# First layer's dilated q and k accumulated in one place, causal q with its cross terms apart: a change to a two-layer hybrid decoder kernel

## The reference, cut to what matters

```
h = rms_norm(x, attn_norm)
proj = h @ w_in
qa, ka, va, qd, kd, vd = jnp.split(proj, [...], axis=-1)
qa = apply_rope(split_heads(qa, N_HEADS_MOBA), cos, sin)
qd = apply_rope(split_heads(qd, N_HEADS_DIL), cos, sin)
x = x + jnp.concatenate([out_a, out_d], axis=-1) @ w_out
x = x + jnp.square(jax.nn.relu(h @ w_up)) @ w_down
```

## Time and profile before

| | us |
|---|---|
| median of three runs | 595.81 |
| profiled execution | 595.47 |
| its span in the trace | 593.7 |
| PE busy in the span | 583.4 (98%) |
| DVE busy | 403.0 (68%) |
| ACT busy | 314.1 (53%) |
| layer 0, step 8 starts | 20.12 |
| layer 0, quad of heads 4 to 7 starts | 57.94 |
| layer 1, the same quad starts | 346.66 |

### The profile page before, as it was taken

How to read it: one execution, slowest core, us unless ns; L and a number is a source line. 1 busy time by engine, 2 the same in 40 slices (tenths; PEclk the granted TensorE clock), 3 DMA queues, 4 the chain that set the end, 5 groups by cost and what they waited for, 6 DMA issues and landing times.

```text
span 593.7 us, 9303 instructions
## 1 busy us (share of the span) xinstructions
PE 583.4 (98%) x3350; PEld 491.6 (83%) x3350; DVE 403.0 (68%) x650; ACT 314.1 (53%) x532; POOL 61.8 (10%) x67
## 2 busy tenths in 40 slices
PE   8989999999999999999999999999999999999995
PEld 6869977788888888888888888778888888888884
DVE  5795987688755755755388968768775755656634
ACT  5746767475535435435185646774645435435322
POOL 0060240210000000000004214102000000000001
PEclk9999999999999999999999999999999999999999
DMA  8946352448665465564255625441876465564301
GB/s 305 368 145 212 106 177 76 139 142 275 221 217 206 148 220 198 154 249 163 71 174 181 213 98 187 143 142 44 270 243 223 151 229 185 158 235 172 107 0 71
DMA packets 58844, 104.20 MB, mean 176 GB/s; under 512 B 1808, under 2 KB 35136, under 8 KB 58816
## 3 DMA queue, kind: packets, MB, share of 16 engines
q1 hardware_dynamic: 58320, 103.03, 51.6%
q10 hardware_dynamic: 496, 0.81, 0.5%
HBM read 102.79 MB, written 1.05 MB: 175 GB/s over the span
## 4 chain that ended last, share of the span: by engine, by line
PE 92%; DMA 3%; DVE 3%; issue 1%; ACT 0%; POOLq 0%; ACTq 0%; POOL 0%; DVEq 0%; SPq 0%
PE psum L1172 20%; PE psum L955 16%; PE psum L957 16%; PE psum L956 16%; PE psum L1175 10%; PE psum L976 5%; DMA raw<-in_w_in 3%; PE psum L981 3%; PE psum L1107 2%; PE psum L1127 2%; PE psum L1145 1%; PE psum L962 1%; DVE w_lo L670 1%; PE psum L1148 1%; DVE rope_b L736 0%
## 5 line engine op out<-in xcount | busy, mean ns | idle before, releaser
L670 DVE TENSOR_TENSOR w_lo<-raw,w_hi 128x1024 fp32r<-128x1024 f32 x188 | 227.2, 1242 | 51.3 <-ACT w_hi L498 51.3
L498 ACT CAST w_hi<-raw 128x1024 fp32r<-128x1024 f32 x188 | 186.7, 1048 | 1.7 <-DMA raw<-in_w_in 1.2
L1172 PE MATMUL psum<-xt,w_hi 128*128 128x512 f32 x512 | 160.7, 395 | 0.0
L955 PE MATMUL psum<-w_hi,ot_hi 128*128 128x512 f32 x320 | 127.0, 397 | 0.0
L956 PE MATMUL psum<-w_lo,ot_hi 128*128 128x512 f32 x320 | 124.8, 390 | 0.0
L957 PE MATMUL psum<-w_hi,ot_lo 128*128 128x512 f32 x320 | 124.8, 390 | 0.0
L1175 PEld LDWEIGHTS psum<-xt,w_lo 128*128 128x128 f32 x512 | 96.2, 188 | 22.4
L1175 PE MATMUL psum<-xt,w_lo 128*128 128x256 f32 x512 | 100.6, 278 | 0.0
L1172 PEld LDWEIGHTS psum<-xt,w_hi 128*128 128x128 f32 x512 | 80.2, 189 | 2.4
L614 ACT COPY up_cross<-psum 128x512 f32<-128x512 f32 x32 | 18.8, 587 | 118.8 <-PE psum L1175 118.8
L846 DVE TENSOR_TENSOR up_cross<-psum,up_cross 128x512 f32<-128x512 f32 x32 | 22.1, 691 | 74.1 <-ACT up_cross L614 74.1
(11 more groups left out here) (98 smaller groups left out, 609.3 us busy)
## 6 DMA issues: line engine op xcount, KB each, us to landing
raw<-in_w_up SPq DMA_DIRECT2D x32, 1024.0 KB, 5.5
raw<-in_w_down SPq DMA_DIRECT2D x32, 1024.0 KB, 6.8
raw<-in_w_in SPq DMA_DIRECT2D x21, 1024.0 KB, 5.2
raw<-in_w_out SPq DMA_DIRECT2D x8, 1024.0 KB, 4.9
raw<-in_w_in SPq DMA_DIRECT2D x3, 512.0 KB, 7.9
raw<-in_w_in SPq DMA_DIRECT2D x4, 256.0 KB, 4.7
out<-x SPq DMA_DIRECT2D x3, 256.0 KB, 2.4
x<-in_x SPq DMA_DIRECT2D x2, 256.0 KB, 4.4
```

The source lines that it names most:

```text
L498: act.copy(dst, src).then_inc(hi_done, 1)
L670: dve.tensor_tensor(lo_t, src, hi_t, ALU.subtract).then_inc(split_done, 1)
L955: pe.matmul(out, s_hi, m_hi, start=first, stop=False)
L1172: pe.matmul(up_banks[b][:, f, :], w_hi[:, slot, cols[f]], xt[:, k, :, :].rearrange("p a b -> p (a b)"), start=k == 0, stop=False)
```

## The change

Layer 0's groups 0 and 1 (dilated q and k) are accumulated in one place: three matmuls of 256 columns a tile and k (`together`), no copies of cross terms, no `add_cross`, rope products straight from PSUM. Layer 1's groups 0 and 1 stay as they were. Group 3 (causal q) has its cross terms apart in both layers: 512 and 256 columns into banks 0 and 1 for half 0, 2 and 3 for half 1, with a copy by ACT and an `add_cross` by DVE at steps 28 and 32.

What moves with it: the row of 1/rms is turned at step 9 into bank 7 instead of at step 11 into bank 0; rope products of dilated q go to steps 10 and 12, of causal q from 28 and 32 to 29 and 33; head 5 is masked at step 30 instead of 31, and so turned at 33 instead of 34; heads 4 and 5 are scored in banks 0 and 1 instead of 1 and 2; two `hi` of ACT come earlier (31 to 29, 32 to 30). PE's waits change with the banks.

```diff
-QK_STEPS = [19, 21, 23, 25, 29, 31, 33, 35, 43, 44, 45, 46, 48, 49, 50, 51]
+QK_STEPS = [19, 21, 23, 25, 29, 30, 33, 35, 43, 44, 45, 46, 48, 49, 50, 51]
...
-CROSS_AT = {8: ((0, 0), (0, 1)), 12: ((1, 0),), 16: ((1, 1),), 36: ((4, 0),), 40: ((4, 1),)}
-SUM_AT = {8: (0, 0), 9: (0, 1), 14: (1, 0), 16: (1, 1), 36: (4, 0), 40: (4, 1)}
-ROPE_ROW = 11
-ROPE_AT = {12: (0, 0), 13: (0, 1), 14: (1, 0), 17: (1, 1), 28: (3, 0), 32: (3, 1), 37: (4, 0), 41: (4, 1)}
+LATER_CROSS = {28: ((3, 0),), 32: ((3, 1),), 36: ((4, 0),), 40: ((4, 1),)}
+CROSS_AT = [LATER_CROSS, {8: ((0, 0), (0, 1)), 13: ((1, 0),), 16: ((1, 1),)} | LATER_CROSS]
+LATER_SUMS = {28: (3, 0), 32: (3, 1), 36: (4, 0), 40: (4, 1)}
+SUM_AT = [LATER_SUMS, {8: (0, 0), 9: (0, 1), 14: (1, 0), 16: (1, 1)} | LATER_SUMS]
+ROPE_ROW = 9
+ROPE_AT = {10: (0, 0), 12: (0, 1), 14: (1, 0), 18: (1, 1), 29: (3, 0), 33: (3, 1), 37: (4, 0), 41: (4, 1)}
...
-HI_LATE = {28: 3, 30: 2}
-HI_AT = {s + HI_LATE.get(s, int(s % 8 in (0, 4))): s // 2 + HI_AHEAD for s in range(0, 2 * ATT_UNITS, 2)}
+HI_AT = {s + int(s % 8 in (0, 4)): s // 2 + HI_AHEAD for s in range(0, 2 * ATT_UNITS, 2)}
...
-            return banks[(1, 2, 4, 5)[h % 4]]
+            return banks[(1, 2, 4, 5)[h % 4] - int(h in (4, 5))]
...
-            warm_up(4)
-            for n in range(4):
-                pe.matmul(banks[n][:, :], squares[:, 0, BANK:BANK + P], squares[:, 1, 0:BANK], start=True, stop=False)
+            warm_up(8)
...
-            def half_in_one_bank(hg, i, k, slot):
-
-                out = group_bank(3, hg)[:, i * SEQ:(i + 1) * SEQ]
-                return three(out, feature_tile(w_hi, k, slot, hg, i), feature_tile(w_lo, k, slot, hg, i),
-                             xt[:, k, 0, :], xt[:, k, 1, :], k == 0, k == KT - 1)
+            def together(g, k, slot, hg, i):
+
+                return three(qk_banks(g, hg)[:, i, 0:SEQ], feature_tile(w_hi, k, slot, hg, i),
+                             feature_tile(w_lo, k, slot, hg, i), xt[:, k, 0, :], xt[:, k, 1, :], k == 0, k == KT - 1)
...
-                    if g == 2 and half == 0:
+                    if g == 1 and half == 1:
                         pe.wait_ge(rope_scaled, l + 1)
+                    elif g == 2:
+                        pe.wait_ge(rope_terms, qk_half(l, 0, half) + 1)
                     elif g == 3:
                         pe.wait_ge(v_done, l * 4 + half + 1)
+                        pe.wait_ge(masked, l * N_HEADS + half + 1)
+                    elif g == 4 and half == 0:
+                        pe.wait_ge(masked, l * N_HEADS + 6)
                     elif g == 4:
-                        pe.wait_ge(rope_terms, qk_half(l, 3, half) + 1)
-                        pe.wait_ge(masked, l * N_HEADS + 4 + half + 1)
+                        pe.wait_ge(acc_summed, APART[l, 3, 1] + 1)
                     elif g == 5:
-                        pe.wait_ge(acc_summed, l * len(SUMMED) + SUMMED[4, half] + 1)
+                        pe.wait_ge(acc_summed, APART[l, 4, half] + 1)
...
+                    elif (l, g, half) in APART:
+                        last = both_tiles(g, k, slot, half)
                     else:
-                        last = both_tiles(g, k, slot, half)
+                        for i in range(2):
+                            last = together(g, k, slot, half, i)
...
+                if h == 4:
+                    pe.wait_ge(acc_summed, APART[l, 3, 0] + 1)
...
             def attention(l, s):
                 if s == ROPE_ROW:
                     pe.wait_ge(rstd_done, l * STATS + ST_X + 1)
-                    pe.wait_ge(acc_summed, l * len(SUMMED) + 1)
```

More of the change, by code:

```diff
@@ L567, in _ @@
                                        scale=rstd[:, ST_X, t:t + 1]).then_inc(v_done, 1)
-                    for g, hg in CROSS_AT.get(s, ()):
+                    for g, hg in CROSS_AT[l].get(s, ()):
                         if g > 0 and hg == 0:
@@ L802, in _ @@
                         norm(l, NORM_AT[s])
-                    if s in SUM_AT:
-                        add_cross(l, *SUM_AT[s])
+                    if s == ROPE_ROW:
+                        scale_rope(l)
+                    if s in SUM_AT[l]:
+                        add_cross(l, *SUM_AT[l][s])
                     if s in ROPE_AT:
-                        if s == min(ROPE_AT):
-                            scale_rope(l)
                         rope_products(l, *ROPE_AT[s])
@@ L938, in _ @@
             pe.sem_inc(pv_done, 4)
-            pe.wait_ge(ones_set, 2)
+            pe.wait_ge(ones_set, 1)
             def warm_up(n):
@@ L1005, in first_project_in @@
                     pe.matmul(qk_banks(0, hg)[:, i, 0:SEQ], feature_tile(w_hi, k, slot, hg, i), xt[:, k, 0, :],
-                              start=False, stop=False)
+                              start=k == 0, stop=False)
                 if k % 2 == 0:
@@ L1011, in first_project_in @@
                 for hg, i in tiles:
-                    with_lo(0, k, slot, hg, i)
+                    pe.matmul(qk_banks(0, hg)[:, i, 0:SEQ], feature_tile(w_lo, k, slot, hg, i), xt[:, k, 0, :],
+                              start=False, stop=False)
                 pe.wait_ge(turned_lo, k + 1)
                 for hg, i in tiles:
-                    last = pe.matmul(qk_banks(0, hg)[:, i, SEQ:2 * SEQ], feature_tile(w_hi, k, slot, hg, i),
+                    last = pe.matmul(qk_banks(0, hg)[:, i, 0:SEQ], feature_tile(w_hi, k, slot, hg, i),
                                      xt[:, k, 1, :], start=False, stop=False)
@@ L1025, in project_in @@
                 half, j = s % 8 // 4, s % 4
-                if half == 0 and g == 3 and j < 2:
-                    unit_ready(l, 2 * g + j, 1)
-                elif half == 0 and g != 3:
+                if half == 0:
                     unit_ready(l, 2 * g + j // 2, j % 2)
                 if j == 0:
-                    if g == 2 and half == 0:
+                    if g == 1 and half == 1:
                         pe.wait_ge(rope_scaled, l + 1)
+                    elif g == 2:
+                        pe.wait_ge(rope_terms, qk_half(l, 0, half) + 1)
                     elif g == 3:
                         pe.wait_ge(v_done, l * 4 + half + 1)
+                        pe.wait_ge(masked, l * N_HEADS + half + 1)
+                    elif g == 4 and half == 0:
+                        pe.wait_ge(masked, l * N_HEADS + 6)
                     elif g == 4:
-                        pe.wait_ge(rope_terms, qk_half(l, 3, half) + 1)
-                        pe.wait_ge(masked, l * N_HEADS + 4 + half + 1)
+                        pe.wait_ge(acc_summed, APART[l, 3, 1] + 1)
                     elif g == 5:
-                        pe.wait_ge(acc_summed, l * len(SUMMED) + SUMMED[4, half] + 1)
[L1040 to L1048, removed]
+                        pe.wait_ge(acc_summed, APART[l, 4, half] + 1)
                 slot = (2 * g + j // 2) % RING
@@ L1073, in first_group @@
                 slot = u // 2 % RING
-                both_tiles(0, k, slot, 0)
-                if k > 0:
+                if l == 0:
+                    for hg in range(2):
+                        for i in range(2):
+                            last = together(0, k, slot, hg, i)
+                elif k > 0:
+                    both_tiles(0, k, slot, 0)
                     last = both_tiles(0, k, slot, 1)
                 else:
+                    both_tiles(0, k, slot, 0)
                     with_both(0, k, slot, 1, 1, True)
```

25 lines of the change are left out of this document (12 added, 13 removed).

## The result

The changed kernel takes **597.59 us** (median of seven runs, 597.43 to 597.82), the kernel before 595.81 in seven runs beside it (595.32 to 595.92). The ratio is 1.0032, 95% interval 1.0023 to 1.0041: slower by 1.8 us, and by more than the 0.2% that runs can tell from none. The profiled execution took 597.56 with a span of 595.8; before, 595.47 with 593.7. So between the two traces there are 2.1 us to find.

What follows compares the result with a forecast made beforehand. PE, busy 98% of the span, was taken to bound the kernel with its few waits. The terms −0.28 − 1.92 − 0.32 + 3.62 + 0.40 gave +1.50 us, forecast 597.3 us (0.25% slower), range 594.2 to 599.5, its own 596.5 to 598.3.

Steps and rivals of the forecast that it cites:

- Term 4: Step 32, both layers: PE waits for DVE's mask of head 5, +1.81 us a layer, +3.62 in all.
- high bound: Wait at step 32: 0.55 us more a layer if POOL's rope sum holds the split up; not taken.
- Term 2: Layer 0, step 19: PE's wait for DVE's low part of unit 11 goes, −1.92 us.
- Terms 1 and 3: Layer 0: slower pitches of dilated q and k, +0.46 us; late restart at step 11's turned row goes, −0.32.
- Term 1: Matmul pitches, 0.0115 us a pair: causal q gains 0.74, layer 0's dilated q and k lose 0.46; net −0.28 us.
- Term 5: Turning head 5 after step 33: PE waits for ACT's copy of head 4, +0.2 us a layer, +0.4.
- Head 6: Later turnings (heads 6, 7): chained as ready 0.6 us or more before PE asks, so no cost.
- the wait does not bind: Rival, step 32, both layers: new wait and turning cost nothing, 593.3 us, faster; chance 0.12.
- binds by half: Rival: wait at step 32 and turning cost 1.0 to 1.6 us a layer, 595.3 to 596.5; chance 0.15.
- Layer 0's wait: Rival: unit 11 or step 12's scaled tables still hold PE in layer 0, 599.2 us; chance 0.08.
- The granted clock: Rival: the clock falls at the new waits, costing a few us; chance 0.02.
- More is late in groups 3 and 4: Rival: DVE, POOL sums and heads 6 and 7 late, up to 1 us a layer, 598.3 to 599.3; chance 0.12.

Runs made afterwards that it cites:

- Experiment 1: Changed kernel with causal q's rope products back at steps 28 and 32 instead of 29 and 33; 595.10 us, ratio 0.9994 to the kernel before.
- experiment 6: Changed kernel with group 3 (causal q) as before the change in both layers, only the dilated part kept; 593.97 us, ratio 0.9970.
- Experiment 5: Changed kernel with layer 0's dilated q and k as before, turned row and product steps not put back; 600.52 us, ratio 1.0081.
- run 7: Changed kernel with causal q's products at 28 and 32, head 5 masked directly behind head 4, layer 1's second dilated k products at 17; 593.38 us.
- 9: Changed kernel with causal q as before the change and layer 1's second dilated k products at step 17; 593.65 us, ratio 0.9971.
- experiment 4: Changed kernel with layer 1's products of dilated k, half 1, back at step 17 instead of 18; 597.18 us, ratio 1.0036.
- experiment 2: Changed kernel with head 5 masked directly behind head 4 at step 29, ahead of products, split and low parts; 597.30 us, ratio 1.0027.

## Why the prediction was right, and where not

The forecast was 597.3, slower; 597.59 was measured, within the range, slower by 0.32%. The five terms, each by its own step:

- **Term 4, the new wait at step 32: right in place, cause and size.** Forecast was a mask of head 5 done 6.03 after the quad's start; it was 6.02. PE's stall against before was forecast as 6.10 + 0.11 − 4.49 = 1.72 a layer; measured is 1.68 at step 32, and 0.07 in the first pair behind it (61.88 to 62.42 is 0.54, a usual pair start takes 0.47), 1.75. Experiment 1 moved one member of the chain and the wait fell by its length. The high bound (a split held up by POOL) did not come: the split at 59.18 took 1.22.
- **Term 2, the wait for unit 11: right.** It is gone, and gone in experiment 6, which has the dilated part alone. Experiment 5, without it, kept 1.2 us of it. Timeline of DVE, changed kernel, layer 0: the scaled tables, and the splits of units 11 and 12:
```profile
23.39 0.69 DVE L710 TENSOR_TENSOR rope_r<-rope_tab,psum 128x512 f32<-128x512 f32 x1 [0.67 <-PE psum L1116]
...
31.22 2.95 DVE L669 TENSOR_TENSOR w_lo<-raw,w_hi 128x1024 fp32r<-128x1024 f32 x2
```
 The tables start at 23.39, forecast 23.6. The two splits take 2.95 together, so the first is done near 32.7 if they are alike; forecast 32.5 to 34.7.
- **Terms 1 and 3 up to the first quad.** From step 8 to the quad the changed kernel gains 1.94; terms 2 and 3 less the slower pitches of the 32 pairs in between (+0.37) are 1.87. The other eight pairs of term 1 lie in steps 6 and 7 and cost 0.10, as forecast (17.15 to 20.03 is 2.88; before, 17.34 to 20.12 is 2.78). Step 8 comes 0.09 sooner all the same, so what lies ahead of step 6 was 0.19 shorter, where the prediction took 0. The start varies by more than that: PE turns the row between 22.59 and 23.12 in the profiled runs with the dilated part together. So of the 2.03 at the first quad 0.2 may be the execution's own.
- **Term 1, causal q: mis-sized a little.** Forecast 0.0115 for 32 pairs, 0.37 a layer. Measured 0.20 for the 24 pairs ahead of the second quad and 0.08 (run 7 against 9) for the eight behind it: 0.28. Between turnings the distance fell from 3.20 to 3.13, 0.07 for eight pairs instead of 0.09.
- **Term 5, turning head 5: right in kind.** Heads 4 and 5 are turned 1.89 apart; one step and a turning are 3.13 − 1.40 = 1.73, so 0.16 is lost, forecast 0.2. ACT's chain was what PE waited for. Timeline of ACT, changed kernel, against the earlier trace rows:
```profile
62.66 1.03 ACT L499 CAST w_hi<-raw 128x1024 fp32r<-128x1024 f32 x1
...
64.13 0.58 ACT L575 COPY qk_raw<-psum 128x512 f32<-128x512 f32 x1
64.60 0.50 ACT L581 COPY probs_t<-psum 128x384 f32<-128x384 f32 x1
```
 The copy of head 4 ends at 65.10, and PE turns head 5 at 65.24. Head 5's own norm was done long before, at 63.54. Head 6, which I had 0.6 in time, lost some 0.06 too. Its norm, the next row, took 1.34 for two instructions where 0.55 is usual, beside POOL's rope sums that run from 67.28 to 69.63; it is done at 69.78, and PE turns head 6 at 69.84:
```profile
68.44 1.34 DVE L698 TENSOR_SCALAR probs<-probs,row_inv 128x128 f32<-128x128 f32 x2
```
- **What failed: layer 1's groups 0 and 1, costed at nothing.** The section on the change says that they stay as they were, and the sum has no term for them. That holds for PE and ACT's copies, but the one table of products, `ROPE_AT`, serves both layers, and its entry went from 17 to 18. That let a split pass ahead of the products and of POOL's sum: +0.51, shown by experiment 4. This is the rest of the difference: the terms gave +1.50, the traces have +2.10, and +0.51 is most of the 0.60 between them. The two medians lie 1.78 apart, since the profiled execution of before was 0.34 under its median and that of the changed kernel at it. So the forecast came within 0.3 of the median by some luck: against the traces, from which its terms were taken, it was 0.6 short, and the start that was 0.19 sooner hid a part of what was left out.

The rivals: that the wait does not bind, or binds by half, is out by the 1.60 on record twice. Layer 0's wait did not stay. The granted clock stood at 1.00, the upper of its two levels (2.4 GHz), over the new waits. The window around layer 0's (us, busy PE, PEld, DVE, ACT, POOL, PEclk, DMA), answering to the earlier trace rows:
```profile
59.80:62.60 2.80, 1.20 (x8) 0.90 (x7) 2.56 (x10) 1.06 (x5) 1.87 (x2) 1.00 0.00 0
```
The eighth column is the clock; layer 1's window has 1.00 too. DVE was busy for 2.56 of these 2.80 us, against 67% over the span: where it is late, its share of the span says nothing. "More is late in groups 3 and 4" came only as the 0.06 at head 6.

**What stays open.** The 0.19 at the start and the 0.07 from step 8 to the first quad. Whether other banks for heads 4 and 5 would have freed PE of the wait at step 32 was not run. Behind step 32 the layers lose +0.32 and +0.34, of which the first pair (0.07), head 5 (0.16) and head 6 (0.06) are 0.29; the rest is as small as the reading. Why a 512-column matmul with a 256-column one behind it takes 12 ns less than three of 256, no run here separates.

## What to carry to other kernels

When a wait is moved to another bank's owner, chain the waited-for engine's instructions in their new order from the event that releases the first of them, and then chain on to the next things that the same engine is asked for, until its work is on time again: experiment 2 cured the first wait, met the second as reckoned, and a third, of 0.60, that had not been chained. An engine that is idle for 4.87 us ahead of such a chain is the cure, if work that needs nothing from the chain is issued in front of it; that one step of distance was worth 2.5 us, more than anything the new form of matmul can bring. And where a table serves two layers, an edit meant for one is a change in the other: every entry that differs is to be priced in each.

## What the runs showed of the hardware that was not expected

- Which of POOL and DVE starts first decides which gets longer. POOL's sum of 128x256 took 0.74 when it started 0.18 ahead of a DVE instruction with two SBUF inputs, and 1.76 when it started 0.03 behind one. The loss of the other order is smaller: 1.11 instead of 0.69 for DVE's product. The kernel before has the second order too, with 0.72 and 1.11. The smallest lead that still decides was not measured.
- DVE's norms are longer beside POOL too: the pair that takes 0.55 alone took up to 1.34 beside a POOL rope sum. No run here takes POOL's sum away from a norm and nothing else, so the cause is read from the overlap alone.
- Stops of 0.06 to 0.12 us of PE do not show as waits. They show as a longer duration of the first instruction behind them (0.52 and 0.55 instead of 0.49 for a turning) and in the distance of start times.
